# Moving a LayerNorm and splitting its second half in a streaming encoder layer

## The chip, the cores and the metric

The kernel runs on one core of one Trainium2 chip. The metric is the device time of one execution in microseconds (us); lower is better. Five engines run their own instruction lists, each strictly in order, and meet only at semaphores: TensorE (PE; its weight loads are PEld), VectorE (DVE), ScalarE (ACT), GpSimd (POOL) and SyncE (SP), which here only issues DMAs.

## The reference, cut to what matters

One layer works on T = 1088 token rows of width 1024 (1024 of a prompt, 64 of a decoded sample). The sample's rows follow their own states, so between the two parts lie padding columns.

```python
z = rms_norm(x, norm1_g) @ w_in                  # 1536 columns: pooling 512, value 512, gate 512
y_pool = pool_mix(...)                           # window means 2/4/8/16 minus the token, then a 128x128 product
v = value * sigmoid(gate)
h = depthwise_conv31(v) + bias                   # causal, one filter of 31 taps for each channel
h = layer_norm(h, ln_g, ln_b); y_conv = h * sigmoid(h)
x = x + concat(y_pool, y_conv) @ w_out + b_out
hm = rms_norm(x, norm2_g)
x = x + hier_moe(hm, ...)                        # best of 4 groups, then 2 of its 8 experts for each token
y = rms_norm(x, norm_f_g)
```

Every token must have its two experts before the first block of rows can be gathered, because the place of a row within its expert's block depends on the counts of all tiles.

## The kernel before, in words

Tokens lie in the free dimension while channels lie in the 128 partitions: `hc` holds the convolution's output as four channel tiles of all tokens, `u_ext` the pooling columns, `v_ext` the gated values. Tokens are also cut into nine tiles of 128 (the last has 64). All float32 products are done as three products of a rounded part ("high", made by ScalarE) and a rest ("low", made by VectorE or GpSimd).

**Input projection.** Twelve column chunks `j` of `w_in` (`KINDS`: gate and value four times, then four pooling chunks) run on TensorE (`in_proj(j, n)`, three token blocks `n`). For each, ScalarE rounds the weights (`w_high`), GpSimd makes the rest (`w_low`), and the chunk's result is taken by `gate`, `glu` or `pool_in`.

**Convolution.** VectorE does 31 taps over 512 tokens for each of the four channel tiles of the first half (`taps(n, "A", c)`) and for tiles 0 and 3 of the second half (`"B"`). The rest of the second half is done by two engines together in four pieces (`HELPED`): ScalarE makes the term of a tap (`products(h, n)`, a scaled copy into a ring `taps_pr` of three buffers for each piece), and GpSimd adds it (`additions(h, n)`). Piece 0 is tile 1, piece 1 the first 400 columns of tile 2 (one term is 128x400), piece 2 its other 206, piece 3 the sample's 64 columns of tiles 0 and 3. `prod_done` counts terms, `help_done` additions, 31 for each piece. A term from number 4 on waits for the addition three before it.

**Convolution's LayerNorm.** `BLOCKS` has three blocks of tokens: 512, 512 and the sample's 64. For each: `ln_mean` on TensorE (a product with a matrix of 1/512), `ln_center` on VectorE, `ln_square` on ScalarE, `ln_variance` on TensorE, `ln_deviation` (a square root) on ScalarE, `ln_normal` (a reciprocal and a product) on VectorE, `ln_swish` (four Silu) on ScalarE. Block 0 is done around the end of the projection, block 1 only after the second half's convolution, when `help_done` has reached 93 (`3 * TAPS`) and VectorE has ended its taps.

**Output projection.** For tile `t`, `out_conv(t)` and `out_pool(t)` (24 products of 512 columns each; called half tiles below) add into `out_ps[t % 2]`. Their operand is made by `mix_conv_high`, `mix_high` (ScalarE) and `mix_conv_low`, `mix_pool_low` (VectorE, tiles 0 to 3) or `mix_low` (GpSimd, tiles 4 to 8). `bias(t)` on GpSimd adds `b_out` to the residual row that SyncE loads; SyncE loads row `t + 2` only after rows `x2` and `hm` of tile `t` have been made and stored. Then, for each tile: `residual` (VectorE), `row_deviation` (ScalarE), `hm_row` (VectorE), `turn_hm` (TensorE transposes), `hm_turned` (ScalarE copy), `logits` (TensorE), `route` and `count` (VectorE), `ranks` (TensorE), `place` (VectorE). After the last `place`, `slot_table` and `slots` give the index of the first gather; from there the 32 experts follow, two in an iteration of a loop.

**Order of the work.** It is written out by hand, one list for each engine. Around the change ScalarE, VectorE and GpSimd run:

```python
# ScalarE, L732 on
mix_high(4); row_deviation(3); products(3, TAPS - 8)
# GpSimd, L1815 on
additions(3, TAPS - 1)
for t in range(4, NT): mix_low(t); bias(t)
# VectorE, L1475
dve.wait_ge(help_done, 4 * TAPS)
```

Lines that the prediction comes to: L606 the term of a tap (ScalarE), L1775 its addition (GpSimd), L533 and L1713 the high and low part of `w_out`, L660 Silu, L701 the pooling part of tiles 0 and 1, L714 the square root of a row, L872 and L880 the two LayerNorm products, L961 the output projection, L1005 `turn_hm`, L1016 `logits`, L1290 `ln_center`, L1297 and L1300 `ln_normal`, L1312 `difference` (window mean minus token), L1366 `residual`, L1378 `hm_row`, L1796 and L1799 `mix_low`, L1807 `bias`.

## Time and profile before

| what | us |
|---|---|
| median of 3 runs | 1085.82 |
| these runs | 1085.67 to 1086.55 |
| the profiled execution's own time | 1086.66 |
| its span, from the first to the last instruction | 1084.80 |
| TensorE busy | 923.5 |
| VectorE busy | 858.9 |
| ScalarE busy | 655.5 |
| GpSimd busy | 312.0 |

The first 130 us are the transposes of the input and eight chunks, the stretch from 130 to 435 us holds the rest of the projection, the convolution's second half, the output projection and the routing, and from 435 us on the experts run. In a timeline row the first number is the start, the second the length, "x24" the number of instructions merged, and the bracket says how long the engine was idle before it and which instruction released it.

### The profile page before, as it was taken

Reading aid. Unit: us, or ns where it says so; the run is one execution under the profiler, and the core shown is the slowest. Engines: PE = TensorE matmul, PEld = TensorE weight load, DVE = VectorE, ACT = ScalarE, POOL = GpSimd, SP = SyncE. Lnnn points to the kernel's source line nnn. Section 1 sums busy time; section 2 is a strip of 40 time slices with the busy share of each in tenths; the row PEclk is TensorE's granted clock in tenths of the full one; section 3 lists DMA queues with packets and bytes.
Section 4 is the critical chain, followed back from the end, with each engine's and each line's share of the span. In section 5 each row is a group of like instructions: output and inputs, shape, how many; then the busy total and the mean of one; then the engine's idle time right before and its main releaser. Section 6 shows DMA issues by size and latency. Waiting matters only on the chain.

```text
span 1084.8 us, 13573 instructions
## 1 busy us (share of the span) xinstructions
PE 923.5 (85%) x4446; PEld 776.5 (72%) x4446; DVE 858.9 (79%) x971; ACT 655.5 (60%) x698; POOL 312.0 (29%) x354
## 2 busy tenths in 40 slices
PE   4999998586468886569999999999999999999920
PEld 4999986364357665458888888888888888888820
DVE  5699996679245737689989898989898989898657
ACT  6425434845633104357888787877787878778515
POOL 3128987776252200102111111111111111112010
PEclk8999999898778785679999999999999999999965
DMA  8211110213115240579999999999999999999877
GB/s 262 85 55 56 42 63 0 81 59 116 59 39 194 88 155 20 190 262 359 381 373 390 384 387 381 402 383 396 374 395 369 389 375 380 377 385 381 303 241 272
DMA packets 67532, 268.64 MB, mean 248 GB/s; under 512 B 15359, under 2 KB 28159, under 8 KB 42921
## 3 DMA queue, kind: packets, MB, share of 16 engines
q1 hardware_dynamic: 57993, 250.36, 62.5%
q0 software_dynamic: 9504, 17.85, 4.3%
q8 instruction: 18, 0.29, 0.1%
q14 instruction: 17, 0.14, 0.0%
HBM read 254.09 MB, written 30.86 MB: 263 GB/s over the span
## 4 chain that ended last, share of the span: by engine, by line
PE 72%; POOL 9%; ACT 6%; DVE 5%; issue 4%; DMA 3%; SPq 0%; POOLq 0%; DVEq 0%; ACTq 0%
PE ps L1111 11%; PE ps L1113 11%; PE ps L1112 11%; PE ps L961 7%; POOL arena L1775 7%; PE ps L1125 6%; PE ps L1126 6%; PE ps L1127 6%; PE ps L1100 3%; PE ps L833 2%; PE ps L1016 2%; PE ps L835 2%; PE ps L834 2%; ACT arena L606 2%; PE ps L1132 1%
## 5 line engine op out<-in xcount | busy, mean ns | idle before, releaser
L758 ACT ACTIVATE big<-arena 128x2048 fp32r<-128x2048 f32 x192 | 363.0, 1914 | 70.3 <-PE ps L1127 37.4
L1585 DVE TENSOR_TENSOR low<-arena,big 128x2048 fp32r<-128x2048 f32 x126 | 285.4, 2287 | 40.3 <-ACT big L758 40.3
L1111 PE MATMUL ps<-big,ring 128*128 128x512 f32 x512 | 205.2, 401 | 2.4 <-DVE ring L1590 2.4
L1113 PE MATMUL ps<-big,ring 128*128 128x512 f32 x512 | 201.1, 393 | 0.0
L1585 DVE TENSOR_TENSOR big<-arena,big 128x2048 fp32r<-128x2048 f32 x66 | 151.0, 2289 | 15.6 <-ACT big L758 15.4
L961 PE MATMUL ps<-big,ring 128*128 128x512 f32 (+1 forms) x432 | 113.5, 423 | 30.1 <-POOL ring L1796 23.9
L1265 DVE SCALAR_TENSOR_TENSOR ps<-arena,cols,ps 128x512 f32<-128x512 f32 x168 | 126.9, 755 | 5.7
L961 PEld LDWEIGHTS ps<-big,ring 128*128 128x128 f32 (+1 forms) x432 | 84.3, 198 | 55.1 <-POOL ring L1796 24.2
L1775 POOL TENSOR_TENSOR arena<-arena 128x606 f32<-128x606 f32 (+3 forms) x120 | 107.8, 898 | 40.6 <-ACT arena L606 25.1
L1111 PEld LDWEIGHTS ps<-big,ring 128*128 128x128 f32 x512 | 96.9, 189 | 22.5 <-DVE ring L1590 2.8
L1113 PEld LDWEIGHTS ps<-big,ring 128*128 128x128 f32 x512 | 96.7, 189 | 22.4
L1125 PE MATMUL ps<-big,hT 128*128 128x512 f32 x256 | 103.2, 403 | 10.1 <-DVE hT L1600 10.1
L1849 POOL COPY cur<-s_idx 128x1 uint32 x32 | 11.9, 371 | 323.9 <-ACT arena L776 323.9
L1127 PE MATMUL ps<-big,hT 128*128 128x512 f32 x256 | 102.3, 400 | 0.0
L1112 PE MATMUL ps<-low,ring 128*128 128x512 f32 x256 | 100.7, 394 | 0.0
L1112 PE MATMUL ps<-big,ring 128*128 128x512 f32 x256 | 100.3, 392 | 0.0
L833 PE MATMUL ps<-big,ring 128*128 128x384 f32 (+1 forms) x288 | 96.4, 335 | 3.6 <-DVE big L1209 3.1
L1126 PE MATMUL ps<-low,hT 128*128 128x512 f32 x248 | 98.8, 398 | 0.0
L606 ACT ACTIVATE arena<-arena,cols 128x64 f32<-128x64 f32 (+3 forms) x150 | 70.5, 513 | 45.6 <-POOL arena L1775 45.6
L835 PE MATMUL ps<-big,ring 128*128 128x384 f32 (+1 forms) x288 | 94.8, 329 | 0.0
L834 PE MATMUL ps<-big,ring 128*128 128x384 f32 (+1 forms) x288 | 94.8, 329 | 0.0
L1125 PEld LDWEIGHTS ps<-big,hT 128*128 128x128 f32 x256 | 49.2, 192 | 21.9 <-DVE hT L1600 8.7
(250 smaller groups left out, 1404.7 us busy)
## 6 DMA issues: line engine op xcount, KB each, us to landing
arena<-in_w_eg SPq DMA_DIRECT2D x64, 1024.0 KB, 7.6
arena<-in_w_eu SPq DMA_DIRECT2D x64, 1024.0 KB, 7.1
arena<-in_w_ed SPq DMA_DIRECT2D x64, 1024.0 KB, 7.3
arena<-in_x_prompt SPq DMA_DIRECT2D x16, 512.0 KB, 5.1
y_in<-y_scratch SPq DMA_DIRECT2D x16, 512.0 KB, 8.3
arena<-in_w_in SPq DMA_DIRECT2D x12, 512.0 KB, 4.4
arena<-in_w_out SPq DMA_DIRECT2D x8, 512.0 KB, 3.8
x_scratch<-arena SPq DMA_DIRECT2D x8, 512.0 KB, 2.7
```

Of the source, the lines that this page charges most:

```text
L758: act.activation(we_h[n % RING], raw[n % RING], ACT.Copy).then_inc(high_done, 1)
L833: pe.matmul(out, sh, mh, start=(i == 0), stop=False)
L961: ins = pe.matmul(out_ps[t % 2][0:r, c0:c0 + BANK], sh[t % 2][:, k, 0:r], mv[:, k, c0:c0 + BANK], start=(first and k == rows[0] and i == 0 ...
L1111: pe.matmul(out, part_h[b][:, k, :], wh[:, q, :], start=(k == 0), stop=False)
L1112: pe.matmul(out, part_h[b][:, k, :], wl[:, q, :], start=False, stop=False)
L1113: ins = pe.matmul(out, part_l[b][:, k, :], wh[:, q, :], start=False, stop=(k == KD - 1))
L1125: pe.matmul(out, hT_h[:, k, :], wh[:, q, c0:c0 + BANK], start=(k == 0), stop=False)
L1126: pe.matmul(out, hT_h[:, k, :], wl[:, q, c0:c0 + BANK], start=False, stop=False)
L1127: ins = pe.matmul(out, hT_l[:, k, :], wh[:, q, c0:c0 + BANK], start=False, stop=(k == KF - 1))
L1265: dve.scalar_tensor_tensor(to, v_ext[:, c, a + j:b + j], cols[:, c, j:j + 1], run, ALU.mult, ALU.add).then_inc(conv_step, 1)
L1585: dve.tensor_tensor(we_l[n % RING], raw[n % RING], we_h[n % RING].bitcast(F32), ALU.subtract).then_inc(low_done, 1)
L1775: pool.tensor_tensor(hc[:, c, a:b], hc[:, c, a:b], term, ALU.add).then_inc(help_done, 1)
```

## The change

- `BLOCKS` has four blocks: 512, 256, 256 and 64; `BLOCK_OF` says which block a tile needs. Buffers and PSUM banks follow (`ln_sd`, `sq`, `mean_ps`, `var_ps`), and counts of semaphores go up by one.
- The first block's LayerNorm moves into the last two chunks on all engines: on TensorE `ln_mean(0)` goes behind the first token block of chunk 10 and `ln_variance(0)` behind its third; on ScalarE `ln_deviation(0)`, `ln_swish(0)` and `mix_conv_high(0)` run before the last `pool_in`; on VectorE `difference` and `ln_center` change places with taps. `state_rows(1)` and `turn_state(1)` go one step on.
- Piece 1 of the helped convolution gets a ring of five buffers, so a term waits for the addition five before it. Its terms and additions are spread differently: GpSimd adds 5, then 4 and 6 in steps 10 and 11, then 6, 3 and 6.
- Two of VectorE's groups of taps on tile 3 (8 taps together) move between `wo_low(4)` and `mix_pool_low`.
- Second half: `out_conv(3)` goes before `ln_mean(1)`; the two blocks of 256 are interleaved with tiles 3 to 5. Sixteen terms of piece 3 are made around block 1's norm, and GpSimd adds 15, then makes tile 4's low part, then adds the other 15.
- `logits(t)` and `hm_turned(t)` for tiles 0 to 8 stand elsewhere: ScalarE does `hm_turned(t - 1)` before `row_deviation(t)`, and TensorE does `logits` a half tile further on.

The diff, without unchanged lines and with eight blanks of indentation taken away:

```diff
--- before.py
+++ after.py
...
-    BLOCKS = [(0, BANK), (BANK, BANK), (SEQ, DEC)]
+    BLOCKS = [(0, BANK), (BANK, BANK // 2), (BANK + BANK // 2, BANK // 2), (SEQ, DEC)]
+    BLOCK_OF = [0, 0, 0, 0, 1, 1, 2, 2, 3]
...
-ln_sd = [place("ln_dev", AT_HTR, BANK)[:, :], r_w[:, 0:BANK], r_w[:, BANK:BANK + DEC]]
+ln_sd = [place("ln_dev", AT_HTR, BANK)[:, :], r_w[:, 0:BANK // 2], r_w[:, BANK // 2:BANK],
+         r_w[:, BANK:BANK + DEC]]
...
-sq = [None, r_s2[:, 0:NC * BANK].rearrange("p (c t) -> p c t", c=NC),
-      r_w[:, D:D + NC * DEC].rearrange("p (c t) -> p c t", c=NC)]
-taps_pr = [r_x[:, s * (HW_ - BANK):(s + 1) * (HW_ - BANK)] for s in range(3)] + [
-    r_s2[:, D + s * 256:D + s * 256 + 256] for s in range(3)] + [
-    r_w[:, 2 * D + s * 2 * DEC:2 * D + (s + 1) * 2 * DEC] for s in range(3)]
+sq = [None] + [r_s2[:, i * D:(i + 1) * D].rearrange("p (c t) -> p c t", c=NC) for i in range(2)] + [
+    r_w[:, D:D + NC * DEC].rearrange("p (c t) -> p c t", c=NC)]
+taps_pr = [[r_x[:, s * (HW_ - BANK):(s + 1) * (HW_ - BANK)] for s in range(3)],
+           [r_x[:, s * 400:(s + 1) * 400] for s in range(5)],
+           [r_s2[:, D + s * 256:D + (s + 1) * 256] for s in range(3)],
+           [r_w[:, 2 * D + s * 2 * DEC:2 * D + (s + 1) * 2 * DEC] for s in range(3)]]
...
-mean_ps = [banks(7, 1), banks(2, 1), banks(5, 1)]
-var_ps = [banks(7, 1), banks(5, 1), banks(5, 1)]
+mean_ps = [banks(7, 1), banks(2, 1), banks(2, 1), banks(5, 1)]
+var_ps = [banks(7, 1), banks(5, 1), banks(5, 1), banks(5, 1)]
...
-help_n = {4: ((0, 6),), 5: ((0, 7),), 6: ((0, 7),), 7: ((0, 7),), 8: ((0, 3), (1, 6)), 11: ((1, 6),)}
+help_n = {4: ((0, 6),), 5: ((0, 7),), 6: ((0, 7),), 7: ((0, 7),), 8: ((0, 3), (1, 5))}
...
-            sp.wait_ge(var_done, 3)
+            sp.wait_ge(var_done, 4)
...
-            if j >= 4:
-                act.wait_ge(help_done, h * TAPS + j - 2)
+            ring_h = taps_pr[h]
+            if j > len(ring_h):
+                act.wait_ge(help_done, h * TAPS + j - len(ring_h) + 1)
...
-                    to = taps_pr[3 * max(h - 1, 0) + j % 3]
+                    to = ring_h[j % len(ring_h)]
...
-    for j, (kind, c) in enumerate(KINDS):
-        if j == NCH - 1:
-            ln_deviation(0)
-        if kind == "gate":
-            gate(c)
-        elif kind == "pool":
-            pool_in(c)
-        if j + 2 < NCH:
-            w_high(j + 2)
-        if j == 8:
-            state_rows(0)
-            state_rows(1)
-        if j == 10:
-            ln_square(0)
-        for h, n in help_n.get(j + 1, ()):
-            products(h, n + (made[h] == 0))
...
-        act.wait_ge(mix_done, NC * (min(tok // BANK, 2) + 1))
+        act.wait_ge(mix_done, NC * (BLOCK_OF[t] + 1))
...
-    for k in range(NC):
-        wo_high(k)
-    ln_swish(0)
-    mix_conv_high(0)
-    products(1, 6)
+    for j, (kind, c) in enumerate(KINDS):
+        if kind == "gate":
+            gate(c)
+        elif kind == "pool":
+            pool_in(c)
+        if j + 2 < NCH:
+            w_high(j + 2)
+        for h, n in help_n.get(j + 1, ()):
+            products(h, n + (made[h] == 0))
+        if j == 8:
+            state_rows(0)
+        if j == 9:
+            state_rows(1)
+            products(1, 4)
+            ln_square(0)
+        if j == 10:
+            ln_deviation(0)
+            products(1, 6)
+            ln_swish(0)
+            mix_conv_high(0)
+    wo_high(0)
+    wo_high(1)
...
+    wo_high(2)
+    wo_high(3)
...
-    products(1, 4)
+    products(1, 3)
...
+    products(1, 3)
...
-    products(1, 4)
+    products(1, 3)
...
-    products(1, 4)
+    products(1, 6)
...
-    row_deviation(2)
+    products(3, 8)
...
+    row_deviation(2)
+    ln_deviation(1)
...
-    ln_deviation(1)
-    hm_turned(1)
...
-    products(3, TAPS - 8)
+    ln_square(2)
...
+    ln_deviation(2)
+    ln_swish(2)
+    hm_turned(1)
+    products(3, TAPS - 16)
+    row_deviation(4)
+    mix_high(6)
...
-    row_deviation(4)
...
-    mix_high(6)
-    ln_square(2)
-    ln_deviation(2)
+    ln_square(3)
...
+    mix_high(7)
...
-    ln_swish(2)
-    mix_high(7)
-    for t in range(6, NT):
-        row_deviation(t)
-        hm_turned(t - 1)
-        if t + 2 < NT:
-            mix_high(t + 2)
-    hm_turned(NT - 1)
+    ln_deviation(3)
+    ln_swish(3)
+    hm_turned(5)
+    row_deviation(6)
+    mix_high(8)
+    hm_turned(6)
+    row_deviation(7)
+    hm_turned(7)
+    row_deviation(8)
+    hm_turned(8)
...
-            if j == 9 and n == 0:
+            if j == 9 and n == 1:
...
-            if j == 10 and n == 1:
+            if j == 10 and n == 0:
...
-            if j == NCH - 1 and n == 1:
+            if j == 10 and n == 2:
...
-        for tok, w in BLOCKS[0:2]:
+        for tok, w in ((0, BANK), (BANK, BANK)):
...
-            pe.wait_ge(cen_done, 2)
+            pe.wait_ge(cen_done, 3)
...
-            pe.wait_ge(lnsd_done, 3)
+            pe.wait_ge(lnsd_done, 4)
...
+    out_conv(3)
...
-    out_conv(3)
...
-    logits(0)
+    pe.wait_ge(cen_done, 2)
+    ln_mean(2)
...
+    pe.wait_ge(lnsd_done, 2)
+    ln_variance(2)
+    logits(0)
+    out_pool(4)
+    turn_hm(2)
...
-    turn_hm(2)
-    out_pool(4)
+    out_conv(5)
+    turn_hm(3)
...
-    turn_hm(3)
...
-    pe.wait_ge(lnsd_done, 2)
-    ln_mean(2)
-    out_conv(5)
-    ln_variance(2)
+    pe.wait_ge(lnsd_done, 3)
+    ln_mean(3)
+    out_pool(5)
+    ln_variance(3)
+    turn_hm(4)
...
+    out_conv(6)
+    turn_hm(5)
+    logits(4)
...
-    turn_hm(4)
-    out_pool(5)
-    logits(4)
+    out_pool(6)
...
-    out_conv(6)
...
-    turn_hm(5)
-    out_pool(6)
+    out_conv(7)
+    turn_hm(6)
...
-    out_conv(7)
-    turn_hm(6)
...
-    logits(6)
...
+    turn_hm(7)
+    logits(6)
...
-    turn_hm(7)
...
-    taps(10, "B", 0, 6)
+    taps(5, "B", 0, 6)
+    difference(0)
+    taps(1, "B", 0, 6)
...
-    difference(0)
-    taps(3, "B", 0, 6)
+    taps(5, "B", 0, 6)
...
-    taps(4, "B", 0, 6)
+    taps(5, "B", 0, 6)
+    ln_normal(0)
...
-    ln_normal(0)
+    taps(TAPS - 22, "B", 0, 6)
...
-    taps(5, "B", 0, 6)
+    taps(6, "B", 3)
...
-    taps(3, "B", 0, 6)
+    taps(2, "B", 3)
...
-    taps(8, "B", 3)
...
+    ln_center(1)
...
-    ln_center(1)
+    ln_normal(1)
...
-    ln_normal(1)
...
+    ln_center(2)
+    ln_normal(2)
+    hm_row(3)
+    route(0)
...
-    route(0)
...
-    hm_row(3)
+    residual(4)
+    hm_row(4)
...
-    residual(4)
-    hm_row(4)
-    ln_center(2)
...
+    ln_center(3)
...
-    ln_normal(2)
+    hm_row(5)
+    ln_normal(3)
...
-    place(0)
-    hm_row(5)
-    place(1)
...
+    place(0)
...
+    place(1)
+    hm_row(6)
...
-    hm_row(6)
...
-            term = taps_pr[3 * max(h - 1, 0) + j % 3]
+            term = taps_pr[h][j % len(taps_pr[h])]
...
+        if step_j >= 10:
+            additions(1, 2 * step_j - 16)
...
-    additions(1, 10)
+    additions(1, 6)
...
-    additions(1, 4)
+    additions(1, 3)
...
-    additions(1, 4)
+    additions(1, 6)
...
-    additions(3, TAPS - 1)
+    additions(3, 15)
...
+        if t == 4:
+            additions(3, TAPS - 16)
...
```

## Rows read from the trace of the kernel before

**Rows 1.** The page: busy time of one engine, its share, its instructions.

```profile
PE 923.5 (85%) x4446; PEld 776.5 (72%) x4446; DVE 858.9 (79%) x971; ACT 655.5 (60%) x698; POOL 312.0 (29%) x354
```

**Rows 2.** Stretches: busy us of PE, PEld, DVE, ACT, POOL; TensorE clock; DMA.

```profile
260.00:308.00 48.00, 24.08 (x97) 16.32 (x97) 17.06 (x16) 32.03 (x82) 20.10 (x34) 0.71 0.19 66
...
388.00:410.00 22.00, 17.89 (x80) 12.50 (x80) 9.01 (x38) 2.35 (x4) 0.00 (x0) 0.84 0.50 191
```

**Rows 3.** Timelines, VectorE, GpSimd: start, length, operation; in brackets idle before it, releaser.

```profile
409.35 1.22 DVE L1366 TENSOR_TENSOR arena<-ps,arena 64x1024 f32<-64x1024 f32 x1 [7.43 <-PE ps L961]
...
434.87 2.29 POOL L1827 DMA_INDIRECT arena<-hm_scratch,g_idx  x1 [13.26 <-DVE g_idx L1522]
```

**Rows 4.** Timeline, TensorE: four places where it waits.

```profile
224.38 7.23 PE L961 MATMUL ps<-big,ring 128*128 128x512 f32 x24 [3.24 <-DVE ring L1337]
...
259.62 6.34 PE L872 MATMUL ps<-arena,mean_w 128*128 128x512 f32 x8 [8.76 <-POOL arena L1775]
...
307.81 8.08 PE L961 MATMUL ps<-big,ring 128*128 128x512 f32 x24 [23.92 <-POOL ring L1796]
...
369.34 3.63 PE L1016 MATMUL ps<-w_rt,arena 128*128 128x36 f32 x16 [5.07 <-ACT arena L680]
```

**Rows 5.** Timeline, ScalarE, from the last chunk to the first tiles.

```profile
185.17 0.80 ACT L578 ACTIVATE arena<-ps 128x768 f32<-128x768 f32 x1
...
186.36 3.93 ACT L533 ACTIVATE big<-arena 128x1024 fp32r<-128x1024 f32 x4
190.31 1.28 ACT L660 ACT_TABLE_LOAD   x1
191.60 2.93 ACT L660 ACTIVATE arena<-arena,cols 128x512 f32<-128x512 f32 x4
...
222.05 1.13 ACT L701 ACTIVATE ring<-arena 128x512 fp32r<-128x512 f32 x2
```

**Rows 6.** Timeline, VectorE, around the first LayerNorm.

```profile
154.95 7.09 DVE L1265 SCALAR_TENSOR_TENSOR ps<-arena,cols,ps 128x512 f32<-128x512 f32 x9
163.04 2.29 DVE L1290 TENSOR_TENSOR arena<-arena,ps 128x2048 f32<-128x2048 f32 x1 [0.99 <-PE ps L872]
165.24 1.30 DVE L1312 SCALAR_TENSOR_TENSOR arena<-arena 128x1103 f32<-128x1103 f32 x1
...
185.31 3.35 DVE L1297 RECIPROCAL ln_dev<-ln_dev 128x512 f32<-128x512 f32 x1 [5.03 <-ACT ln_dev L636]
```

**Rows 7.** Timeline, TensorE: the first block's means at full clock.

```profile
159.41 3.59 PE L872 MATMUL ps<-arena,mean_w 128*128 128x512 f32 x8
```

**Rows 8.** Timeline, GpSimd, the same stretch.

```profile
211.31 4.43 POOL L1775 TENSOR_TENSOR arena<-arena 128x400 f32<-128x400 f32 x4
215.69 4.79 POOL L1713 TENSOR_TENSOR big<-arena,big 128x1024 fp32r<-128x1024 f32 x2
```

**Rows 9.** Timeline, VectorE: the row of the second tile.

```profile
259.43 4.13 DVE L1378 SCALAR_TENSOR_TENSOR arena<-arena,stat,g_bc 128x1024 f32<-128x1024 f32 x1
```

**Rows 10.** Timeline, SyncE: the load of the fourth tile's residual.

```profile
263.95 0.43 SPq L432 DMA_DIRECT2D arena<-in_x_prompt  x1
```

**Rows 11.** Timeline, GpSimd, between the second and the fifth tile.

```profile
259.43 2.34 POOL L1807 TENSOR_TENSOR arena<-arena,bo_bc 128x1024 f32<-128x1024 f32 x1
268.59 4.06 POOL L1807 TENSOR_TENSOR arena<-arena,bo_bc 128x1024 f32<-128x1024 f32 x1 [6.82 <-DMA arena<-in_x_prompt]
...
293.56 13.05 POOL L1775 TENSOR_TENSOR arena<-arena 128x128 f32<-128x128 f32 x23 [17.06 <-ACT arena L606]
306.57 1.18 POOL L1796 TENSOR_TENSOR ring<-arena,ring 128x512 fp32r<-128x512 f32 x1
```

**Rows 12.** Timeline, TensorE: a half tile, one tile's logits, a transposed row.

```profile
266.59 5.74 PE L961 MATMUL ps<-big,ring 128*128 128x512 f32 x24
...
281.11 1.87 PE L1016 MATMUL ps<-w_rt,arena 128*128 128x36 f32 x16
282.81 1.07 PE L1005 MATMUL ps<-ident,arena 128*128 128x128 f32 x8
```

## Prediction

> **What bounds the kernel now.** I read the page first: TensorE is busy 923.5 us of 1084.8 [rows 1], so about 161 us are its waits. The table of stretches puts them between 182 and 435 us: in 260 to 308 TensorE is busy 24.1 of 48 us at a mean clock of 0.71, and even in a stretch of the last tiles, 388 to 410, it has 17.9 of 22 at 0.84 while no other engine is busy for half of it [rows 2]. From 435 us on the experts run on their own; nothing there changes and I carry that part over whole. So the question is how early the first gather starts: before, at 434.87 [rows 3]. TensorE's timeline names what it waits for [rows 4]: VectorE's pooling part of tile 0 (3.2 us), GpSimd's last addition of piece 2 ahead of the second LayerNorm (8.8), GpSimd's low part of tile 4 (23.9), and in the last tiles the copy of the transposed row (5.1, the longest of four such stops, the others 3.7 to 3.8). I follow the four places in turn. Times called "new" are worked out, not measured.
>
> **First place, up to the pooling parts of tiles 0 and 1: 10.6 us.** Before, ScalarE makes them at 222.05 [rows 5], behind the last term of piece 1, which waits for GpSimd's additions; these waited for windows, and the windows for VectorE's `difference`. ScalarE stood in that queue too, so `ln_deviation(0)` and the last `pool_in` (185.17) came late, and VectorE idled 5.0 us before its reciprocal at 185.31 [rows 6].
>
> New order on VectorE: the first half's taps end as before at about 154.2. Then five taps of 0.79 (7.09 / 9), `difference` 1.4, a tap, `ln_center` 2.2, five taps, `difference`, five taps, reciprocal and product 3.4 + 2.2, the product being of `ln_center`'s size [rows 6]: 23.2 us, so 177.4. The waits inside end earlier: means (3.5 us at full clock [rows 7]) from 154.3 to 157.8, VectorE needs them at 160.3; the variance is done near 168.5 and its root near 169.2, needed at 171.8. TensorE loses nothing: the two small products move, and its old stop for `state_rows` becomes one of about 2 us for the taps.
>
> ScalarE: table load 1.28 before 177.4, Silu 2.9, high part 0.6, last `pool_in` 1.2: 182.5, against 186.4 before [rows 5]. That `pool_in` now stands behind the norm; since the chunk ends only near 180, this costs about 1.3 us. Then four `wo_high` (3.9), two `pooled` (2.1, each the size of a `wo_high`), a high part and the first term: near 189.8. From there GpSimd has 15 additions and three low parts of 2.4 each (4.79 / 2). An addition costs 1.11 (4.43 / 4) [rows 8]; I take 1.2, for those that fall beside VectorE. That ends at 215; the last term follows the fourth addition from the end by 0.5, so both pooling parts start near 211.5 to 212, against 222.05: 10.6 us earlier. Bounds: 14 if every addition costs 1.11 and none meets VectorE, 5 if ScalarE's new order is late by as much as it gains in `pool_in`.
>
> The 8 taps moved on tile 3 fill VectorE's idle time before the pooling parts; their former place was hidden behind TensorE's half tile (7.23 us [rows 4]), so I cost them at nothing. If the norm or `pooled` came late they would cost up to 6.3.
>
> **Second place, from the second norm to tile 4: 18.4 us.** The stretch from there to 259.62 keeps its length, so piece 2 ends at 248.9. Moving `out_conv(3)` ahead of the wait fills 5.5 us of TensorE's 8.8, but the end is GpSimd's. Now the chain: ScalarE has made terms 0 to 3 of piece 3 and stops at number 4, since the ring of three wants the first addition. GpSimd gets to that only after `bias(3)`, whose row SyncE loads only after `hm_row(1)`. This is a new wait: behind it in ScalarE's queue stand `hm_turned(0)` and `ln_square(1)`, which before came ahead of the terms. `hm_row(1)` takes 4.1 [rows 9], to 252.9; from its end to `bias(3)` 5.0 pass, the load among them (263.56 to 268.59) [rows 9 to 11]; `bias` 2.3 undisturbed [rows 11]: 260.3. One addition 0.57 (13.05 / 23) and four terms: 263.1. Then `hm_turned(0)` and the square, 1.0 each by their size; the variance on 256 columns by a TensorE that has idled: half of 6.34 [rows 4], with its start 3.5: 268.6; the root 0.5; eight terms 4.4, while VectorE normalises in 2.9 (half of 5.6 and the start); table load 1.3, four Silu on 256 columns 2.1 (between half of 2.9 and all of it), high part 0.6, low part 1.2 [rows 5, 11]: `out_conv(4)` at 278.7. From 248.9 that is 29.8; before, from 259.62 to 307.81, it was 48.2 [rows 4]. Bounds: 12, if `bias(3)` costs 4.06 as before [rows 11] and the Silu are not cheaper than 2.9 and the terms wait for each addition; 28, if the load is back before GpSimd asks, which takes 9 of ScalarE's stop away.
>
> **Third place, tiles 4 to 8: 12.4 us.** Before, from 307.81 to 409.3, 101.5 us for ten half tiles. A half tile takes 5.6 at full clock, one tile's logits 1.7 (281.11 to the next start at 282.81), a transposed row 0.9 net of overlap [rows 12]. New: `out_conv(4)` 5.6, variance 1.7, logits 1.7, half tile 5.6, row 0.9, logits 1.7: 295.9. Then a new stop: `out_conv(5)` needs tile 5's low part, which GpSimd makes after its second 15 additions. Their terms come after block 2's Silu and `hm_turned(1)` (285.8 + 0.5 + 2.9 + 2.1 + 1.0 = 292.3); 15 of 0.57 and 1.2 for the low part [rows 11] with 0.6 of steps give 302.7, a stop of 6.8. `out_conv(5)` then runs from a slow start in 7.2, like the 7.23 after a stop [rows 4]: 309.9. VectorE waits for the same additions, with tile 4's residual behind it; that is late but not last. From there TensorE has seven half tiles 39.2, five logits 8.5, five rows 4.5, block 3's two products 1.7, six `ranks` 2.4, and one stop of 1.6 where `place(1)` stands behind a residual: 57.9, so 367.8. Gone is the stop of 5 us per tile, since `hm_turned` no longer waits behind the residual of the next tile. VectorE was busy 9.0 of 22 us in such a stretch [rows 2], so its share fits. 89.1 against 101.5. Bounds: nothing, if each tile again takes its 22 us; 19, without the stop for additions.
>
> **Tail: 1.5 us.** From the last residual to the gather it was 25.5 (409.35 to 434.87) [rows 3]; VectorE's list there is unchanged, and it loses only its wait for logits(7), now ready. Bounds 0 and 2. SyncE still issues the experts' first weights at tiles 5 and 8, and ScalarE needs them only after tile 8's last half; with some 55 us between I cost their loads at nothing, and at 2 the other way should one be late.
>
> **Sum.** 10.6 + 18.4 + 12.4 + 1.5 = 42.9. Against the profiled execution's own 1086.66: 1043.8. That execution was 0.84 above the median, so **1043**.
>
 By that rule the sum would be that of the first rival below, 1046; by the rows of the additions alone it is the forecast.
>
> **The rivals.**
> - *GpSimd is blocked in its chain.* The first and second place now hang on GpSimd's additions while VectorE makes low parts of the weights. If each of five such VectorE operations (1.2 us each, a part already in my 1.2) stops an addition, 3 us are lost: 1046. The pairs above [rows 9, 11] speak for it; against it, the additions of 1.11 were beside VectorE's taps.
> - *The last tiles keep their pace*, because VectorE's new order (residuals between two `place`) puts a wait where the copy's wait was. The third place and the tail give nothing: 1043 + 13.9 = 1057. For it, VectorE's long lists in single file; against it, its low busy share.
> - *ScalarE's stop at term 4 is short*: the residual's load is back early; 9 to 10 us more: 1033. Against it, 5.0 measured from `hm_row(1)` to `bias(3)`.
> - *The first place gives nothing*, since the last `pool_in` behind the norm delays all that follows: 1054.
> - *Slower: TensorE stays at the lower clock.* Before, its clock fell to 0.71 in a stretch with stops [rows 2]. If the new stops (in front of the second norm, of its variance and of tile 5) held it at 1.2 instead of 2.4 GHz, each of 11 half tiles would take 5.6 more, twice its length [rows 3], and seven logits 1.7 each: 74 us, 1117. It decides from eight slow half tiles on. Against it, in the stop-and-go of 388 to 410 the clock was 0.84.
>
> **Chances.** Forecast 0.64; blocked GpSimd 0.12; last tiles 0.12; short stop 0.06; no first place 0.03; slow clock 0.03. The range 1030 to 1060 takes in all but the last, with 3 us either way for the unseen half-size operations. Faster by over 0.2% (2.2 us, about what a measurement of this kernel can tell from no change) 0.96, within it 0.01, slower 0.03.
>
> **What would show it.** Right: the pooling parts of tiles 0 and 1 near 212; a gap of some 10 us in ScalarE between the fourth and fifth pair of piece 3's terms, ended by GpSimd; `out_conv(4)` near 279; a stop of about 7 us in TensorE ahead of `out_conv(5)`, released by GpSimd's low part; the last half tile ending near 368, the gather near 392; an unchanged length from there. Wrong: a stop above 10 us elsewhere in TensorE, a stretch of the last tiles still at 22 us a tile, or a wait of the first expert block for weights.

## The result, and the profile after

| what | before | after |
|---|---|---|
| median, us | 1085.74 | 1058.56 (1054.73 to 1060.60) |
| ratio to before, 95% interval | | 0.9745 (0.9713 to 0.9776) |
| profiled execution, us | 1086.66 | 1056.91 |
| its span, us | 1084.80 | 1055.20 |

The change gains 27 us where 43 were forecast; 1058.56 lies in the range of 1030 to 1060 by 1.4 us, and two of its four runs took 1060.2 and 1060.6. The profiled execution is 1.65 us below the median, so the table by places, which is made from it, adds up to 29.6. Both spans can be cut at the same five events, so that each place of the prediction gets its measured length:

| place, from and to | before | forecast gain | after | gain |
|---|---|---|---|---|
| 1: start to the end of piece 2 (`ln_mean(1)`) | 259.62 | 10.6 | 255.76 | 3.9 |
| 2: to `out_conv(4)` | 48.2 | 18.4 | 29.1 | 19.1 |
| 3: to the last residual | 101.5 | 12.4 | 98.0 | 3.5 |
| tail: to the first gather | 25.5 | 1.5 | 24.0 | 1.5 |
| experts: to the end | 649.9 | 0 | 648.4 | 1.5 |
| sum | 1084.8 | 42.9 | 1055.2 | 29.6 |

The cuts are these rows of the TensorE, VectorE and GpSimd timelines of the changed kernel. They answer [rows 3, 4]; lines 888 and 977 are the old 872 and 961.

```profile
255.76 1.97 PE L888 MATMUL ps<-arena,mean_w 128*128 128x256 f32 x8 [2.00 <-POOL arena L1798]
...
268.99 3.78 PE L896 MATMUL ps<-arena,mean_w 128*128 128x256 f32 x8 [10.38 <-ACT arena L637]
...
284.84 8.05 PE L977 MATMUL ps<-big,ring 128*128 128x512 f32 x24 [3.93 <-POOL ring L1821]
...
311.42 8.41 PE L977 MATMUL ps<-big,ring 128*128 128x512 f32 x24 [6.92 <-POOL ring L1821]
...
321.02 1.06 PE L1021 MATMUL ps<-ident,arena 128*128 128x128 f32 x8 [1.19 <-ACT arena L669]
...
351.19 7.34 PE L977 MATMUL ps<-big,ring 128*128 128x512 f32 x24
```

```profile
382.87 1.22 DVE L1387 TENSOR_TENSOR arena<-ps,arena 64x1024 f32<-64x1024 f32 x1 [2.92 <-PE ps L977]
```

```profile
406.83 2.29 POOL L1854 DMA_INDIRECT arena<-hm_scratch,g_idx  x1 [11.72 <-DVE g_idx L1545]
```

ScalarE's new wait at the fifth pair of piece 3's terms, which the forecast put at some 10 us, is there too:

```profile
264.78 2.30 ACT L612 ACTIVATE arena<-arena,cols 128x64 f32<-128x64 f32 x8 [8.85 <-POOL arena L1798]
```

The 23.9 us of TensorE ahead of `out_conv(4)` have become 10.4 and 3.9, and the stop ahead of `out_conv(5)` is there with 6.92 us (forecast 6.8). But `out_conv(4)` takes 8.05 us where 5.6 were taken, `out_conv(5)` 8.41 where 7.2 were, and `ln_variance(1)` 3.78. The stretches of the same trace (columns as in [rows 2]) say why:

```profile
255.80:284.80 29.00, 14.73 (x64) 12.04 (x64) 11.71 (x9) 15.39 (x39) 16.02 (x19) 0.79 0.32 108
284.80:311.40 26.60, 19.66 (x96) 16.70 (x96) 8.22 (x19) 16.53 (x44) 11.09 (x19) 0.82 0.12 42
...
343.00:382.70 39.70, 37.42 (x195) 29.14 (x194) 31.18 (x142) 7.87 (x12) 6.07 (x4) 0.96 0.43 162
```

From 343 us on TensorE is busy 37.4 of 39.7 us at 0.96, where [rows 2] had 17.9 of 22: the last tiles are now bound by TensorE, as forecast. The loss lies ahead of that, in the first two rows: TensorE is idle for a half and a quarter of the time, and its mean clock is 0.79 and 0.82.

The page's busy times answer [rows 1]:

```profile
PE 913.7 (87%) x4462; PEld 773.3 (73%) x4462; DVE 867.9 (82%) x974; ACT 657.9 (62%) x706; POOL 320.4 (30%) x354
```

TensorE idles 141.5 us of the span instead of 161. VectorE and GpSimd are busy 9.0 and 8.4 us longer, with only three instructions more on VectorE and none on GpSimd: the same work takes longer.

In place 1 the rows of GpSimd, VectorE and ScalarE answer [rows 5, 6, 8]:

```profile
177.58 9.79 POOL L1798 TENSOR_TENSOR arena<-arena 128x400 f32<-128x400 f32 x6 [0.24 <-POOL fix L1776]
...
192.97 9.95 POOL L1798 TENSOR_TENSOR arena<-arena 128x400 f32<-128x400 f32 x6 [3.05 <-ACT arena L612]
...
205.23 4.38 POOL L1798 TENSOR_TENSOR arena<-arena 128x400 f32<-128x400 f32 x3
...
214.20 7.70 POOL L1798 TENSOR_TENSOR arena<-arena 128x400 f32<-128x400 f32 x6
```

```profile
154.60 2.89 DVE L1285 SCALAR_TENSOR_TENSOR ps<-arena,cols 128x512 f32<-128x512 f32 x1
...
168.66 1.90 DVE L1332 SCALAR_TENSOR_TENSOR arena<-arena 128x1103 f32<-128x1103 f32 x1
170.59 0.90 DVE L1335 COPY arena<-fix 128x7 f32<-128x7 f32 x1
...
178.60 2.29 DVE L1320 TENSOR_TENSOR arena<-arena,ln_dev 128x2048 f32<-128x2048 f32 x1
180.81 2.15 DVE L1332 SCALAR_TENSOR_TENSOR arena<-arena 128x1103 f32<-128x1103 f32 x1
```

```profile
215.80 1.14 ACT L711 ACTIVATE ring<-arena 128x512 fp32r<-128x512 f32 x2
```

An addition of 400 columns takes 1.63, 1.66, 1.46 and 1.28 us in the four groups, where I took 1.2 and [rows 8] had 1.11. These are means of two kinds. Narrower windows part the first group:

```profile
178.78 5.07 POOL L1798 TENSOR_TENSOR arena<-arena 128x400 f32<-128x400 f32 x2
```

```profile
183.99 3.38 POOL L1798 TENSOR_TENSOR arena<-arena 128x400 f32<-128x400 f32 x3
```

The second and third addition last 3.02 and 1.91 us, beside the norm's product and `difference`, which both read two inputs from SBUF; the last three, beside taps whose running sum lies in PSUM, last 1.03 each. In the whole stretch from 150 to 222 us 11 of 25 additions last 1.3 us or more, each beside a VectorE instruction with two inputs in SBUF; the other 14 last 1.02 to 1.06. Before, from 178 to 225 us, only 4 of 24 were held like that, up to 1.91. VectorE is held too: its first tap, the one whose running sum still lies in SBUF, takes 2.89 us where the same tap took 0.76 before, and a copy of seven columns 0.90, where one of 15 columns just before took 0.17. The pooling parts start at 215.80, not at 212.

### The profile page after: what moved, and what is told of

It reads as the page before. It is cut to its first block, busy times and chain, and to the rows that moved or that the text cites. A ratio compares the mean times of both kernels' runs of the same rounds, so it can differ in the third digit from the quotient of the medians.

```text
span 1055.2 us, 13619 instructions
## 1 busy us (share of the span) xinstructions
PE 913.7 (87%) x4462; PEld 773.3 (73%) x4462; DVE 867.9 (82%) x974; ACT 657.9 (62%) x706; POOL 320.4 (30%) x354
## 4 chain that ended last, share of the span: by engine, by line
PE 59%; DVE 8%; ACT 3%; issue 2%; DMA 2%; POOL 1%; SPq 0%; DVEq 0%; POOLq 0%; ACTq 0%
PE ps L1131 11%; PE ps L1133 11%; PE ps L1132 11%; PE ps L1145 6%; PE ps L1146 6%; PE ps L1147 6%; PE ps L1120 3%; PE ps L977 3%; PE ps L1152 1%; DMA y_in<-y_scratch 1%; ACT arena L612 1%; DVE arena L1675 1%; DMA arena<-hm_scratch,g_idx 1%; PE ps L1032 1%; PE ps L896 1%
## 5 line engine op out<-in xcount | busy, mean ns | idle before, releaser
L977 PE MATMUL ps<-big,ring 128*128 128x512 f32 (+1 forms) x432 | 116.3, 432 | 23.9 <-POOL ring L1821 10.9
L1798 POOL TENSOR_TENSOR arena<-arena 128x606 f32<-128x606 f32 (+3 forms) x120 | 116.7, 972 | 41.0 <-ACT arena L612 25.5
L977 PEld LDWEIGHTS ps<-big,ring 128*128 128x128 f32 (+1 forms) x432 | 87.7, 206 | 48.8 <-POOL ring L1821 11.2
```

What stands on the lines that cost most here:

```text
L977: ins = pe.matmul(out_ps[t % 2][0:r, c0:c0 + BANK], sh[t % 2][:, k, 0:r], mv[:, k, c0:c0 + BANK], start=(first and k == rows[0] and i == 0 ...
L1798: pool.tensor_tensor(hc[:, c, a:b], hc[:, c, a:b], term, ALU.add).then_inc(help_done, 1)
```

## The experiments

Ratios are to the kernel before on the same chip. There were three further chips: one for the halves and the four moved terms, one for the three experiments after that, one for the last three. On the second of these the changed kernel itself ran again.

> The changed kernel again, on the chip of the three that follow, so that they are compared with it and not only with the kernel before. Expected: 0.9745 of the kernel before, within 0.003; the terms of the trace within 1 us of the first one (end of piece 2 at 255.8, out_conv(4) at 284.8, last half tile ended at 382.7, gather at 406.8).

1055.58 us, ratio 0.9715 (0.9693 to 0.9736). Against 0.9745 that is 3 us for one and the same kernel: between runs on different chips a difference of that size decides nothing, and the traces have to. Cut as above it has 255.35 for the end of piece 2, 26.8 to `out_conv(4)` (282.10), and the gather at 404.11; so from `out_conv(4)` on the times are 2.6 to 2.7 us off where 1 was expected, and place 2 varies by 2.3 us from one execution to the next. The trace shows where: the row for `bias(3)` is loaded behind `hm_row(1)`, which ended 1.7 us after piece 2 in the first trace and 0.5 before that in the second.

### Each half of the change alone

The first kernel has only the moved first norm, piece 1's ring of five and what belongs to them, with the second half of the kernel before; the second kernel the reverse. The core of the first, against the changed kernel:

```diff
-    BLOCKS = [(0, BANK), (BANK, BANK // 2), (BANK + BANK // 2, BANK // 2), (SEQ, DEC)]
+    BLOCKS = [(0, BANK), (BANK, BANK), (SEQ, DEC)]
...
-            products(3, 8)
             hm_turned(0)
...
-            additions(3, 15)
+            additions(3, TAPS - 1)
             for t in range(4, NT):
```

> Only the first half of the change: the first LayerNorm inside the last chunks, the ring of five buffers, GpSimd's new spread of additions; the second half's order and its three blocks are as before. Theory A, the prediction's sum: the pooling parts of tiles 0 and 1 come 10.6 us earlier and all of it reaches the end, so 1075 us. Theory B, GpSimd and VectorE block each other: in the changed kernel these parts came at 215.8 instead of 222.05, and the end of piece 2 at 255.6 instead of 259.5; with the same loss here only about 4 us reach the end, 1081 to 1082 us.

> Only the second half of the change: two blocks of 256 tokens, 15 and 15 additions around tile 4, the new places of logits and hm_turned; the first LayerNorm and the rings are as before. Theory A and theory B agree on most of it: from the end of piece 2 to the fifth tile's first half 19 us (48.2 to 29.1 in the two traces), in the last tiles 4 to 12. Additive halves (the 27.2 us of the whole less what the first half gives): 1062.5 us if the first half gives 4, 1069 if it gives 10.6.

The first half alone gave 1081.46 us, 0.9942 (0.9923 to 0.9961), some 6 us: theory B. The second alone gave 1062.86 us, 0.9782 (0.9763 to 0.9801), some 24. Together 30, where the whole gave 28 and 31 by its two ratios: the halves add up within the doubt, and what is missing of the 43 is missing inside each. In the trace of the second, place 2 is 29.3 long. In the trace of the first, GpSimd's additions are as slow as in the full change (9.65 for six) and piece 2 ends at 255.61, 4.0 earlier than before. So place 1's 10.6 was too high by itself, without anything of the second half.

### Which stop costs what: four terms moved behind the norm

ScalarE makes terms 0 to 3 of piece 3, then the copy, the square and `ln_deviation(1)`, and the other 12 behind it, so that nothing stands behind term 4.

```diff
-            products(3, 8)
+            products(3, 4)
             hm_turned(0)
             ln_square(1)
             row_deviation(2)
             ln_deviation(1)
-            products(3, 8)
+            products(3, 12)
             ln_swish(1)
```

> The changed kernel, with ScalarE's terms 4 to 7 of piece 3 moved behind hm_turned(0), ln_square(1), row_deviation(2) and ln_deviation(1), so that the wait for the first addition no longer holds the second norm up. Theory A, the stop at term 4 is on the path that sets the start of tile 4: out_conv(4) starts at 277 instead of 284.8 and the kernel takes 1050.5 us. Theory C, GpSimd's chain (bias(3), 15 additions, low part of tile 4) sets that start by itself: out_conv(4) no earlier than 283 and 1057 us.

1055.04 us, 0.9714 (0.9687 to 0.9740), which its time can't tell from the changed kernel. `out_conv(4)` starts at 278.18, near theory A's 277, but piece 2 also ended 1.8 us sooner; neither theory has its time. In the trace place 2 is 24.2 us long: the variance starts 6.6 us after the mean instead of 13.2, but `out_conv(4)` follows only 17.6 us later instead of 15.9. ScalarE shows what took the place:

```profile
264.22 2.97 ACT L612 ACTIVATE arena<-arena,cols 128x64 f32<-128x64 f32 x12
267.87 0.59 ACT L612 ACTIVATE arena<-arena,cols 128x64 f32<-128x64 f32 x2 [0.68 <-POOL arena L1798]
269.94 2.88 ACT L612 ACTIVATE arena<-arena,cols 128x64 f32<-128x64 f32 x10 [1.48 <-POOL arena L1798]
```

Twelve terms (24 instructions) at the pace of the additions now stand between the root and the Silu. A stop taken away by order alone moved part of the wait.

### GpSimd and VectorE kept apart

VectorE's low parts of `w_out` and of the operands of tiles 0 and 1 are replaced by copies of the same size out of its own PSUM bank; these low parts are left out of the product. The routing becomes another with that, so only the trace up to the gather is comparable, not the time (1196.81 us). VectorE also got a few waits for its own earlier instructions.

```diff
-                dve.tensor_tensor(wo_l[:, WO_ROWS[k], :], wo_raw[k % 4], wo_h[:, WO_ROWS[k], :].bitcast(F32),
-                                  ALU.subtract).then_inc(wl_dve, 1)
+                dve.wait_ge(conv_step, steps[0])
+                dve.tensor_scalar(wo_l[:, WO_ROWS[k], :].rearrange("p (a n) -> p a n", a=2),
+                                  acc_ps.unsqueeze(1).to_broadcast([P, 2, BANK]), 1.0, None, ALU.mult).then_inc(wl_dve, 1)
```

> The changed kernel, with VectorE's low parts of w_out (wo_low) and of the operands of tiles 0 and 1 replaced by copies of the same size from its own PSUM bank, so that they read no SBUF; the low parts of these are left out of the product. Theory B (VectorE's operations with two inputs in SBUF and GpSimd's additions of 400 columns hold each other up): the additions beside them fall from 1.6 to 1.1 or 1.2 us, the pooling parts of tiles 0 and 1 start at 211 to 212 instead of 215.8, piece 2 ends near 251.5, and the time is 3.5 to 4.5 us under the changed kernel's. Theory D (ScalarE's and TensorE's order sets the place, the additions only fill it): the pooling parts stay at 215 to 216 and the time within 1 us of the changed kernel's.

GpSimd in this kernel, and in the changed one on the same chip:

```profile
177.09 9.81 POOL L1812 TENSOR_TENSOR arena<-arena 128x400 f32<-128x400 f32 x6 [0.24 <-POOL fix L1790]
...
193.34 8.05 POOL L1812 TENSOR_TENSOR arena<-arena 128x400 f32<-128x400 f32 x6 [3.90 <-ACT arena L612]
...
211.76 6.97 POOL L1812 TENSOR_TENSOR arena<-arena 128x400 f32<-128x400 f32 x6
```

```profile
193.41 10.08 POOL L1798 TENSOR_TENSOR arena<-arena 128x400 f32<-128x400 f32 x6 [4.45 <-ACT arena L612]
...
213.80 7.72 POOL L1798 TENSOR_TENSOR arena<-arena 128x400 f32<-128x400 f32 x6
```

With the same number of VectorE instructions in the same places, but without two inputs from SBUF, six additions fall from 10.08 to 8.05 and from 7.72 to 6.97. Of these 15 additions one still lasts longer than 1.05 us, 2.13, beside the last `difference`, which was left as it is. The group at 177 keeps its 9.81: beside it stand VectorE's norm and another `difference`, left as they are too. The pooling parts start at 213.36 instead of 215.42, piece 2 ends at 252.89 instead of 255.35. That is 2.5 us, where theory B put 3.5 to 4.5 and D nothing: B's mechanism, some two thirds of its size.

### TensorE kept busy in its waits

Products of 512 columns that nobody reads go into a free PSUM bank, 32 in all:

```diff
+            spin(7)
             pe.wait_ge(wl_dve, NC)
             out_conv(0)
...
+            spin(3)
...
+            spin(11)
             ln_variance(1)
...
+            pe.wait_ge(lnsd_done, 2)
+            spin(4)
             out_conv(4)
...
+            pe.wait_ge(lnsd_done, 3)
+            spin(7)
             out_conv(5)
```

> The changed kernel, with products nobody reads (32 in all, of 512 columns, into a free PSUM bank) put into five of TensorE's waits: before out_conv(0), out_conv(1), ln_variance(1), out_conv(4) and out_conv(5). Theory E (what follows these waits is slow because TensorE's clock has fallen during them): out_conv(0) 8.4 to 5.6, ln_variance(1) 3.8 to 1.9, out_conv(4) 8.05 to 5.6 and out_conv(5) 8.4 to 5.6, of which the last three stand on the path: 7 us under the changed kernel's time, 6 if out_conv(0) gives nothing. Rival F (the slow starts are of other origin, such as operands read late or weights loaded late, or they lie beside other waits): the four durations stay within 0.5 us, or they fall and the time stays within 1.5 us of the changed kernel's.

The granted clock (the number behind the five busy times) in the changed kernel, in stretches that hold `ln_variance(1)`, `out_conv(4)` and `out_conv(5)` alone, and then for the same three with the extra products:

```profile
268.90:272.20 3.30, 3.21 (x8) 2.59 (x9) 0.00 (x0) 1.37 (x4) 0.00 (x0) 0.50 0.00 0
284.80:292.80 8.00, 7.96 (x25) 6.37 (x26) 0.00 (x0) 3.85 (x7) 3.46 (x2) 0.69 0.02 6
...
311.40:319.80 8.40, 8.38 (x24) 6.34 (x24) 5.44 (x6) 3.60 (x6) 3.70 (x3) 0.66 0.15 62
```

```profile
268.50:270.10 1.60, 1.60 (x10) 1.38 (x8) 0.00 (x0) 0.00 (x0) 0.00 (x0) 1.00 0.00 0
282.50:288.20 5.70, 5.70 (x25) 4.70 (x26) 0.00 (x0) 3.81 (x7) 3.46 (x2) 1.00 0.00 0
306.80:312.50 5.70, 5.68 (x24) 4.43 (x24) 4.69 (x4) 0.87 (x1) 3.49 (x2) 1.00 0.01 5
316.40:321.60 5.20, 5.12 (x25) 5.15 (x25) 3.62 (x18) 0.00 (x0) 2.94 (x3) 0.50 0.56 202
```

Of the clock's two levels 0.50 is 1.2 GHz and 1.00 is 2.4 GHz. In the changed kernel TensorE had been idle for 10.4, 3.9 and 6.9 us ahead of these three; the first runs at 0.50 throughout, the others at a mean between the levels. Theory E holds for the durations: with the waits filled 0.50, 0.69 and 0.66 become 1.00, and 3.78, 8.05 and 8.41 us become 1.89, 5.78 and 5.77. The fourth, `out_conv(0)`, took 6.08 us where it had taken 8.44, and 7.10 in the run beside it. For the time theory E fails and the second branch of rival F holds: 1056.28 us, 0.9734 (0.9711 to 0.9757), no gain. Two reasons are in the trace. The 11 products ahead of `ln_variance(1)` ended at 268.5 although its operand was ready at 265.5, so in that place more was lost than gained. And from `out_conv(4)` to `out_conv(5)` 2.6 us were gained (24.3 instead of 26.9), but the next thing was late:

```profile
316.48 1.94 PE L1028 MATMUL ps<-ident,arena 128*128 128x128 f32 x8 [3.89 <-ACT arena L669]
...
323.19 7.23 PE L982 MATMUL ps<-big,ring 128*128 128x512 f32 x24
```

A stop of 1.07 us in the run beside it has become 3.89, and the clock is back at 0.50 behind it. What ends it is `hm_turned(2)` on ScalarE, which stands behind the square of row 4; that waits for `residual(4)`, and VectorE held `residual(4)` and `count(0)` back until the last addition of piece 3. The changed kernel has the same chain, in VectorE's and ScalarE's rows:

```profile
310.27 1.18 DVE L1437 TENSOR_TENSOR arena<-iota,eid 128x64 f32<-128x64 f32 x1 [7.66 <-POOL arena L1798]
...
314.92 1.22 DVE L1387 TENSOR_TENSOR arena<-ps,arena 128x1024 f32<-128x1024 f32 x1
```

```profile
316.17 1.06 ACT L722 ACTIVATE arena<-arena 128x1024 f32<-128x1024 f32 x1 [7.04 <-DVE arena L1387]
```

### The middle in another order

Four terms ahead of the norm, the others between later steps; GpSimd makes the low parts of tiles 4 and 5 between 11 and 19 additions; VectorE's wait ahead of `count(0)` asks for piece 2 only. With that the fourth block's two products on TensorE and its square and centring come a few steps later. From ScalarE's list:

```diff
-            products(3, 8)
+            products(3, 4)
...
             mix_high(5)
+            products(3, 8)
             ln_deviation(2)
-            ln_swish(2)
+            products(3, 7)
             hm_turned(1)
-            products(3, TAPS - 16)
+            ln_swish(2)
```

> The changed kernel with another order in the middle and nothing else: ScalarE makes only terms 0 to 3 of piece 3 before hm_turned(0) and the second block's square, and the others between later steps; GpSimd makes the low parts of tiles 4 and 5 and their bias between 11 and 19 additions; VectorE no longer waits for piece 3 ahead of count(0). Theory G (both stops, 8.9 us of ScalarE ahead of the second norm and 6.9 us of TensorE ahead of out_conv(5), are caused only by where piece 3's terms and additions stand): out_conv(4) starts 14 us earlier against the end of piece 2 than with the changed kernel (15 instead of 29.1 after it), the stop ahead of out_conv(5) is under 2 us, and the time is 17 to 20 us under the changed kernel's. Rival H (other waits stand right behind, VectorE's long lists and the slow clock of TensorE): half of that at most, 6 to 10 us.

1048.81 us, 0.9648 (0.9617 to 0.9679), 6.8 us less than the changed kernel beside it: rival H. Place 2 has 18.1 us, but now the copy `hm_turned(1)` stands behind terms that wait for additions, and TensorE's stop only went to another place:

```profile
272.08 5.74 PE L978 MATMUL ps<-big,ring 128*128 128x512 f32 x24
...
292.24 1.94 PE L1022 MATMUL ps<-ident,arena 128*128 128x128 f32 x8 [5.39 <-ACT arena L669]
```

### The two stops, each by its cause

One kernel gives piece 3 eight buffers instead of three; one puts tile 5's low part ahead of the second additions and takes VectorE's wait from `count(0)`; the third has both, and on ScalarE eight more terms ahead of `ln_deviation(2)` and `hm_turned(2)` ahead of the square of row 4.

```diff
-                   [r_w[:, 2 * D + s * 2 * DEC:2 * D + (s + 1) * 2 * DEC] for s in range(3)]]
+                   [r_w[:, 2 * D + s * 2 * DEC:2 * D + (s + 1) * 2 * DEC] for s in range(8)]]
```

```diff
-            dve.wait_ge(help_done, 4 * TAPS)
+            dve.wait_ge(help_done, 3 * TAPS)
             count(0)
...
                 mix_low(t)
+                if t == 5:
+                    additions(3, TAPS - 16)
                 bias(t)
-                if t == 4:
-                    additions(3, TAPS - 16)
```

> The changed kernel, with a ring of eight buffers instead of three for the terms of piece 3, and nothing else: term 4 then no longer waits for GpSimd's first addition behind bias(3). Theory R (the stop of 8 to 9 us in ScalarE ahead of the second norm comes from the small ring alone): the stop goes, ln_square(1) starts 6 to 7 us after the end of piece 2 instead of 9.8, ln_variance(1) about 7 us instead of 10.9, out_conv(4) 19 to 20 us instead of 26.8 to 29.1, and the time is 6 to 9 us under the changed kernel's (ratio to the kernel before 0.963 to 0.966). Rival S (the terms and additions themselves are the pace, as in the run that only put four terms behind the norm): out_conv(4) 24 us after the end of piece 2, 3 us gained, 0.969.

1049.27 us, 0.9660 (0.9640 to 0.9680): theory R. The ring alone brings place 2 to 19.8 us; the stop ahead of `out_conv(5)` stays.

```profile
255.32 3.75 PE L888 MATMUL ps<-arena,mean_w 128*128 128x256 f32 x8 [8.08 <-POOL arena L1798]
...
262.64 2.81 PE L896 MATMUL ps<-arena,mean_w 128*128 128x256 f32 x8 [2.06 <-ACT arena L637]
...
275.16 5.77 PE L977 MATMUL ps<-big,ring 128*128 128x512 f32 x24 [0.78 <-POOL ring L1821]
...
299.48 8.16 PE L977 MATMUL ps<-big,ring 128*128 128x512 f32 x24 [6.94 <-POOL ring L1821]
```

> The changed kernel, with GpSimd's second 15 additions behind tile 5's low part instead of ahead of it, and VectorE's wait for all additions moved from count(0) to the fourth block's centring, where it stands anyway. Theory T (the stop of 6.9 us ahead of out_conv(5), and VectorE's wait of 7.7 us with residual(4) behind it, cost what they last): out_conv(5) follows tile 4's logits without a stop, residual(4) starts 9 to 10 us earlier, and the last half tile ends about 6 us earlier: 5.5 to 7 us under the changed kernel's time (0.965 to 0.967). Rival U (ScalarE's 15 terms, which hold hm_turned(2) and the square of row 4 back, were the next thing late): a new stop of 3 us or more ahead of turn_hm(3), 2 to 4 us gained (0.968 to 0.970).

1050.50 us, 0.9676 (0.9643 to 0.9708): in time between the two theories, in the trace rival U. The stop is gone, and the one that U named stands behind it, with the slow clock (0.51 in its stretch):

```profile
301.95 5.75 PE L977 MATMUL ps<-big,ring 128*128 128x512 f32 x24
311.59 1.94 PE L1021 MATMUL ps<-ident,arena 128*128 128x128 f32 x8 [3.89 <-ACT arena L669]
...
318.30 7.43 PE L977 MATMUL ps<-big,ring 128*128 128x512 f32 x24
```

> Both of these in one kernel, and on ScalarE eight more terms of piece 3 ahead of ln_deviation(2) and hm_turned(2) ahead of the square of row 4, so that no queue of the second half waits for piece 3. If the two stops are independent, the gains add: out_conv(4) 19 to 20 us after the end of piece 2, out_conv(5) 20 us after out_conv(4) instead of 26.9, the last half tile 13 to 16 us earlier than in the changed kernel, ratio 0.956 to 0.960, some 1040. If something else becomes the pace (VectorE's list, or TensorE's clock after the stops that are left), the ratio stays above 0.962.

1034.45 us (1034.20 to 1036.12), 0.9523 (0.9504 to 0.9543): faster than both kernels, and below what I expected. From `out_conv(4)` to `out_conv(5)` TensorE no longer stops (18.7 us), and the clock is 1.00 from 293 to 329 us:

```profile
253.72 3.65 PE L889 MATMUL ps<-arena,mean_w 128*128 128x256 f32 x8 [1.96 <-POOL arena L1799]
...
274.44 7.25 PE L978 MATMUL ps<-big,ring 128*128 128x512 f32 x24 [2.35 <-POOL ring L1822]
...
293.12 5.75 PE L978 MATMUL ps<-big,ring 128*128 128x512 f32 x24
```

```profile
293.10:328.90 35.80, 33.24 (x194) 28.59 (x194) 25.76 (x97) 14.10 (x24) 13.90 (x10) 1.00 0.50 178
```

By ratio (of 1086 us, with the changed kernel at 0.9715, so with the doubt of 3 us between chips) the parts gain 6.0 and 4.2 us, both together 20.9. That is more than the sum, but the third kernel has a third change, ScalarE's two moved calls, and how much of the 20.9 comes from those was not separated. The traces show what each part alone left: a stop in TensorE of 6.94 us in the one and of 3.89 in the other, with slowed products behind both.

## Why the prediction was right and wrong, step by step

**The order of the waits was right.** Every stop that was forecast is there and is ended by what was named: ScalarE's gap between the fourth and fifth pair of terms (8.85 us, by GpSimd, at 264.78), TensorE's 6.92 ahead of `out_conv(5)`, no stop of 5 us per tile any more, a tail shorter by 1.5. TensorE's 10.38 ahead of `ln_variance(1)` is part of the forecast's own chain, which had 16.2 us from the end of piece 2 to that product (265.1 less 248.9; measured 13.2). The times that were to show it came late all the same: the pooling parts at 215.8 for 212, `out_conv(4)` at 284.8 for 279, the end of the last half tile at 382.8 for 368, the gather at 406.8 for 392. The missing 13 us are in the sizes of place 1 and place 3 (6.7 and 8.9, less some 2 that came elsewhere); the time lies in the range because the range was wide. Slips of 0.2 to 0.4 us in the sums (182.5 for 182.1, 285.8 for 286.0) change nothing.

**Place 1: 6.7 us mis-sized.** The step that failed is "near 189.8. From there GpSimd has 15 additions ... I take 1.2". GpSimd's last 15 additions began at 192.97, 3.2 later, since VectorE's norm ended at 180.9 instead of 177.4 (first tap 2.1 longer, `difference` with its copy 1.3). The second trace shows another limit close by: there the norm ended 1.0 us sooner and the additions began 0.4 later, because ScalarE waited 1.6 us for a product of TensorE. The 15 took 22.0 us instead of 18: seven lasted 1.03 to 1.06, and eight, each beside a VectorE instruction with two inputs in SBUF, 1.30 to 2.02. The 1.11 of [rows 8] was the cheapest of five groups from 178 us on; the others had 1.18 to 1.28, each with one addition held in the same way. So piece 1 ended at 221.9 (214.20 + 7.70) where 215 was forecast and 225.1 was before.

The pooling parts still came 6.25 earlier, because with a ring of five ScalarE runs two more additions ahead of GpSimd: the last term now follows the sixth addition from the end (215.27), and "the fourth addition from the end" is still the distance of the ring of three. For that lead "the stretch from there to 259.62 keeps its length" doesn't hold; GpSimd's 3.2 us went on, and piece 2 ended 3.9 us earlier. Of the 6.7 us, 4.3 are thus the late pooling parts (215.8 for 211.5) and 2.4 the lead that didn't go on.

The cause of the slow additions is shown by a run for those beside the low parts (2.5 us back when VectorE read PSUM). For the two beside the norm and `difference` only the single rows show it, and for VectorE's own delays too (its first tap began 0.01 us behind a GpSimd instruction of 2.35 us); no run took these away.

The first rival, blocked GpSimd, was thus the right one. Its price for one operation held: it took 3 us for five, and the eight additions lost 4.8 us; what it had wrong was the number, and that VectorE loses time too. The rule of the Trainium skill, "SBUF — State Buffer", section "Who interferes with whom", says that a VectorE instruction with two SBUF inputs contends with a GpSimd instruction that reads SBUF. The run that moved VectorE's input to PSUM agrees (10.08 to 8.05).

**Place 2: right in sum, by luck: two errors cancel.** The first addition of piece 3 was done 9.1 us after piece 2's end instead of 12.0. `hm_row(1)` ended 1.7 us after that end instead of 4.1: this time `bias(2)` was the one held (4.00 us) and `hm_row(1)` took 2.02, the other way round than in [rows 9, 11]. So the row was loaded sooner (the third rival, at 3 us instead of 9). But the eight pairs of terms behind the root took 6.3 us instead of 4.4, because two of the eight additions, one beside the norm's product and one beside `hm_row(2)`, took 1.23 and 1.91 us instead of 0.43. The ring run gives the size of the stop itself: 7 to 9 us.

**Place 3: 8.9 us mis-sized.** Against the forecast's own terms: `out_conv(4)` 2.4 more and `out_conv(5)` 1.2 more by the clock, which the forecast knew from [rows 4] (8.08 for the first half tile behind a stop) and did not apply to `out_conv(4)`; a stop of 1.2 ahead of `turn_hm(3)`, of 0.9 ahead of the fourth block's variance, of 1.0 ahead of a later transpose; 1.7 in `out_conv(7)` (7.34, at a clock of 0.76), 0.3 less for `place(1)`. That makes 8.1; the other 0.8 lies in pieces of 0.3 and less (the six `ranks` 2.7 for 2.4, the stop 6.92 for 6.8, the other half tiles a little over 5.6). The sentence that fell is "VectorE waits for the same additions, with tile 4's residual behind it; that is late but not last": as soon as TensorE was faster it was the next thing late, 3.9 us.

**The slow rival had the right mechanism and the wrong size.** The lower clock followed the stops of 10.4, 3.9 and 6.9 us, at a cost of 1.9 to 2.7 us each, and one of 1.3 ahead of `out_conv(7)`; behind the stops of 1.2, 0.9 and 1.0 the next half tile took 5.7 to 5.8. That is far from eight half tiles. (Its half tile of 5.6 us is in [rows 12], not [rows 3].) The last tiles didn't keep their pace either (37.4 of 39.7 us busy), so the second rival, whose time of 1057 is nearest to the measured one, has the wrong cause.

## What to carry to other kernels

A ring that is too small for the work queued behind it turns one engine's delay into a wait of another; a larger ring removed here what a new order removed only in part (place 2 at 24.2 us) or moved elsewhere (a new stop of 5.4). When a stop goes, price the work that follows at the clock that the stop leaves behind, and look at once for the next wait on every engine: two single repairs gave 6 and 4 us, and both in one kernel, with two calls moved for the waits that came next, 21. A duration read where VectorE had at most one input in SBUF is no price for a GpSimd addition beside one with two (1.03 against 1.30 to 3.02 us): count the pairs that will meet, one by one, since the mean of a merged row hides them.

## What the runs showed of the hardware

VectorE and GpSimd hold each other up in both directions, also with tiny operations. `hm_row(1)` and `bias(2)` show both: before, VectorE's took 4.13 us and GpSimd's 2.34; in the changed kernel, where VectorE's began 0.1 us sooner, they took 2.02 and 4.00. In the changed kernel's second trace, VectorE's difference of 128x4 numbers, usually 0.22 us, and GpSimd's addition of a bias row start and end together:

```profile
324.70 2.43 DVE L1427 TENSOR_SCALAR gdif<-lgt,top 128x4 f32<-128x4 f32 x1
```

```profile
324.71 2.40 POOL L1832 TENSOR_TENSOR arena<-arena,bo_bc 128x1024 f32<-128x1024 f32 x1 [3.84 <-DMA arena<-in_x_prompt]
```

How such pairs meet differs from one execution to the next: of the first four `wo_low` two met an addition in one trace of the changed kernel and took 2.06 us, and the other two 1.22; in the other trace all four were through in time and took 1.22. That goes with the spread of its times, 1054.7 to 1060.6 us, while the last kernel's stay within 2 us; that it is the cause was not tested.
